# Three sizes of expert tile, mixing weights split in another stage, and a later split of the S5 rows, in a one-layer hybrid decoder kernel

## The reference

```python
h = rms_norm(x, g_mix); proj = h @ w_in            # q, k, v of 3 head groups | S5 input | gate_a | gate_b
attn = dilated_window_attention(...)               # 3 groups (window 128, 512, 2048; dilation 1, 4, 16), 8 heads of 64
y_a = attn @ w_attn_proj                           # groups combined per position by their softmax denominators
y_s = gelu(s5_ssm(u)); y_s = y_s * sigmoid(y_s @ w_glu + b_glu)
x = x + (sigmoid(gate_a) * y_a + sigmoid(gate_b) * (y_s @ w_ssm_proj)) @ w_out
h2 = rms_norm(x, g_ffn)
top_v, top_i = top_k(h2 @ w_router + b_router, 4)  # 4 of 32 experts for each token
gu = rows_of_expert @ w_gu + b_gu                  # 1024 -> 2 x 1024, per expert
act = min(g, 7) * sigmoid(1.702 * min(g, 7)) * (clip(l, -7, 7) + 1)
x[token] += gate * (act @ w_down + b_down)         # 1024 -> 1024
```

## Time and profile before

| | us |
|---|---|
| median of 3 runs | 5875.7 (5872.85 to 5878.38) |
| the profiled execution | 5878.18, with a span of 5876.5 |
| TensorE busy | 5454.7 (93% of the span) |
| VectorE busy | 3167.2 (54%) |
| ScalarE busy | 1765.4 (30%) |
| GpSimd busy | 990.3 (17%) |

### The profile page before, as it was taken

One profiled execution on the slowest core, in us unless ns is written; L12 is line 12 of the kernel. 1 busy time (PEld: TensorE's weight loads), 2 busy tenths in 40 slices (PEclk: granted clock), 3 DMA queues, 4 the chain that ended last, 5 costly groups with the idle time before them and its releaser, 6 DMA issues.

```text
span 5876.5 us, 81957 instructions
## 1 busy us (share of the span) xinstructions
PE 5454.7 (93%) x30240; PEld 4852.6 (83%) x30240; DVE 3167.2 (54%) x5833; ACT 1765.4 (30%) x2783; POOL 990.3 (17%) x813
## 2 busy tenths in 40 slices
PE   8999999959979986869699999999999999999997
PEld 7888888848857884658699999999999899999997
DVE  4323220016655665535456566565665777777776
ACT  4111111101105672113223233233333343434343
POOL 0000000003300001213213222132221222222222
PEclk9999999975559997989799999999999999999999
DMA  3122122110012334344444445444454666666665
GB/s 135 67 77 74 67 77 74 67 61 1 0 52 107 115 128 165 127 148 143 150 144 154 162 142 175 143 155 167 137 174 143 218 214 215 224 217 219 220 220 191
DMA packets 237817, 803.35 MB, mean 137 GB/s; under 512 B 32534, under 2 KB 52654, under 8 KB 201808
## 3 DMA queue, kind: packets, MB, share of 16 engines
q1 hardware_dynamic: 198960, 673.20, 31.2%
q0 software_dynamic: 32944, 107.67, 8.0%
q10 hardware_dynamic: 5760, 20.45, 1.1%
HBM read 652.88 MB, written 148.94 MB: 136 GB/s over the span
## 4 chain that ended last, share of the span: by engine, by line
PE 45%; DVE 4%; ACT 1%; issue 1%; DMA 0%; POOL 0%; DVEq 0%; ACTq 0%; POOLq 0%
PE ex_g L1905 28%; PE ex_d L1919 15%; DVE ex_y L2050 2%; PE ex_g L1891 1%; ACT ex_wgh L1956 1%; DVE ex_wdl L2008 1%; DVE ex_wgl L2002 1%; DVE ex_t L2029 0%; DVE ex_bgu L2023 0%; POOL ex_y L1863 0%; DMA ex_nxt<-slots_d 0%; DMA ex_xg<-h_d,ex_nxt 0%; ACT ex_xh L1969 0%; POOL out L1866 0%; DVEq L2059 0%
## 5 line engine op out<-in xcount | busy, mean ns | idle before, releaser
L1905 PE MATMUL ex_g<-ex_xh,ex_wgh 128*128 128x256 f32 (+1 forms) x4352 | 1341.3, 308 | 56.9 <-DVE ex_t L2029 49.5
L1905 PE MATMUL ex_g<-ex_xh,ex_wgl 128*128 128x256 f32 (+1 forms) x4352 | 1334.6, 307 | 0.0
L1905 PE MATMUL ex_g<-ex_xl,ex_wgh 128*128 128x256 f32 (+1 forms) x4352 | 1334.0, 307 | 0.0
L1905 PEld LDWEIGHTS ex_g<-ex_xh,ex_wgh 128*128 128x128 f32 x4352 | 820.2, 188 | 87.5 <-issue 57.0
L1905 PEld LDWEIGHTS ex_g<-ex_xl,ex_wgh 128*128 128x128 f32 x4352 | 820.2, 188 | 8.6
L1905 PEld LDWEIGHTS ex_g<-ex_xh,ex_wgl 128*128 128x128 f32 x4352 | 821.1, 189 | 0.0
L2002 DVE TENSOR_TENSOR ex_wgl<-ex_wg,ex_wgh 128x2048 fp32r<-128x2048 f32 x274 | 626.6, 2287 | 55.8 <-ACT ex_wgh L1956 53.5
L1956 ACT ACTIVATE ex_wgh<-ex_wg 128x2048 fp32r<-128x2048 f32 x274 | 524.6, 1915 | 436.0 <-PE ex_g L1905 409.4
L1863 POOL TENSOR_SCALAR ex_y<-ex_y,ex_cur 128x1024 f32<-128x1024 f32 x84 | 298.3, 3551 | 1712.3 <-DVE ex_y L2050 1712.3
L1919 PE MATMUL ex_d<-ex_wdh,ex_ath 128*128 128x512 f32 x1344 | 538.6, 401 | 0.0
L1919 PE MATMUL ex_d<-ex_wdl,ex_ath 128*128 128x512 f32 x1344 | 530.4, 395 | 0.0
(11 more groups left out here) (343 smaller groups left out, 8767.0 us busy)
## 6 DMA issues: line engine op xcount, KB each, us to landing
ex_wg<-in_w_gu SPq DMA_DIRECT2D x276, 1024.0 KB, 4.8
ex_wd<-in_w_down SPq DMA_DIRECT2D x276, 512.0 KB, 5.6
qkv_d<-prj_o SPq DMA_DIRECT2D x144, 256.0 KB, 2.0
att_blk<-qkv_d SPq DMA_DIRECT2D x48, 768.0 KB, 4.2
prj_raw<-in_w_in SPq DMA_DIRECT2D x112, 256.0 KB, 3.7
ex_bd<-in_b_down SPq DMA_DIRECT2D x34, 512.0 KB, 6.6
gate_d<-prj_o SPq DMA_DIRECT2D x64, 256.0 KB, 2.0
mix_ring<-gate_d SPq DMA_DIRECT2D x32, 512.0 KB, 3.7
```

Of the source, the lines that this page charges most:

```text
L1905: last = pe.matmul(gu[j][:, 0:size], w[:, k, j, :], x[:, k, 0:size], start=(k == 0 and x is xh and w is h), stop=(k == KD - 1 and w is l))
```

## The change

There are three parts.

1. **Experts.** A third tile size, MIDDLE = 320. An expert's rows are cut into large tiles as long as more than 512 remain beyond them. Of the rest, over 384 gives two tiles of 256, 321 to 384 one of 384, 257 to 320 one of 320, up to 256 one of 256. The table has one more column (the first tile of the third kind), each engine loads one more number and runs three loops. In a middle tile the gate-up product and the elementwise work on its result have 320 columns; everything counted in groups of 128 rows has three groups, as in a large tile.
2. **Mixing weights.** The ten pieces are loaded, copied and subtracted during attention: SyncE issues a load in every second block, behind the load of a block, and GpSimd makes the high and the low part in the odd blocks, behind the copy of kT. The six weight tiles live from attention to the end of mixing. The ring, ScalarE and VectorE have no weight pieces in the mixing stage any more, the first chunk's order is written anew, and the loads of attention results are issued ahead of the S5 rows.
3. **S5 rows.** In the mixing chunks `split_y(c + 1)` moves on VectorE from ahead of column block 0 to ahead of column block 3, and on ScalarE behind the second save.

The diff, cut: the same edits (a third loop, `n0, n1, n`, `TW` for 4) repeat on the other engines; waits on the weight pieces are dropped in `glu`, `product` and the ring.

```diff
-LARGE, SMALL = 384, 256
+LARGE, MIDDLE, SMALL = 384, 320, 256
 NGT = LARGE // P
 REGION = -(-S // LARGE) * LARGE
 SLOTS = NE * REGION + LARGE
 DUMP = S + LARGE
+TW = 5
...
+                    if n % 2 == 0 and n // 2 < len(pieces):
+                        r = n // 2
+                        if r >= PR:
+                            sp.wait_ge(low, r - PR + 1)
+                        sp.dma_start(raw[r % PR][:, :], pieces[r][0]).then_inc(raw_in[r % PR], 16)
                     g, row, step, _ = blocks[n]
                     sp.wait_ge(o_saved, n + 1)
                     sp.dma_start(att_d[g, row:row + (P - 1) * step + 1:step, :],
@@ -923,6 +932,13 @@
                         if n:
                             pool.wait_ge(s_mm, PB * n)
                         pool.tensor_copy(kT[(n + 1) % 2][:, :, 0:P], kT[n % 2][:, :, P:2 * P]).then_inc(k_kept, 1)
+                    if n % 2 and n // 2 < len(pieces):
+                        r = n // 2
+                        _, h, l = pieces[r]
+                        pool.wait_ge(raw_in[r % PR], 16 * (r // PR) + 16)
+                        pool.tensor_copy(h, raw[r % PR][:, :]).then_inc(high, 1)
+                        pool.wait_ge(high, r + 1)
+                        pool.tensor_tensor(l, raw[r % PR][:, :], h.bitcast(F32), ALU.subtract).then_inc(low, 1)
...
-                def load_piece(n):
-                    src, k = pieces[n][2:]
-                    if n >= GR:
-                        sp.wait_ge(wl_ready, n - GR + 1)
-                    src = src[:, k:k + 2, :] if n < KA // 2 else src[:, k, :].rearrange("p (h n) -> p h n", h=2)
-                    sp.dma_start(ring[n % GR][:, :, :], src).then_inc(ring_in[n % GR], 16)
                 def load_gates(t):
                     c, o = divmod(t, NO)
-                    r = (NP + t) % GR
-                    if t < GR:
-                        sp.wait_ge(wl_ready, NP + t - GR + 1)
-                    else:
+                    r = t % GR
+                    if t >= GR:
...
+                load_att(0)
                 load_y(0)
-                load_piece(0)
-                load_piece(1)
-                load_att(0)
                 load_att(1)
                 sp.dma_start(bg[:, :], b_glu).then_inc(bg_in, 16)
-                for n in range(2, NP):
-                    load_piece(n)
...
+                turn(0)
                 glu(0)
-                for n in range(NBLK):
+                for n in range(1, NBLK):
...
+                weigh(0)
                 split_y(0)
-                split_weights(0)
-                split_weights(1)
                 act.wait_ge(bg_in, 16)
-                weigh(0)
-                for n in range(2, 4):
-                    split_weights(n)
+                weigh(1)
+                save(0)
                 gate(0)
-                weigh(1)
-                for n in range(4, NP):
-                    split_weights(n)
-                save(0)
                 weigh(2)
                 save(1)
                 weigh(3)
                 save(2)
                 save(3)
                 for c in range(NCH - 1):
-                    split_y(c + 1)
                     weigh(NBLK * (c + 1))
                     for j in range(NBLK):
                         if j + 1 < NBLK:
                             weigh(NBLK * (c + 1) + j + 1)
                         save(NBLK * (c + 1) + j)
+                        if j == 1:
+                            split_y(c + 1)
                     gate(c + 1)
             @block.vector
             def _(dve):
                 tt = dve.tensor_tensor
-                def split_weights(n):
-                    dve.wait_ge(wh_ready, n + 1)
-                    tt(piece(1, n), ring[n % GR][:, :, :].rearrange("p k n -> p (k n)"), piece(0, n).bitcast(F32),
-                       ALU.subtract).then_inc(wl_ready, 1)
...
+                combine(0)
                 split_y(0)
-                split_weights(0)
-                split_weights(1)
-                combine(0)
-                for n in range(2, 4):
-                    split_weights(n)
+                combine(1)
+                save(0)
                 gate(0)
-                combine(1)
-                for n in range(4, NP):
-                    split_weights(n)
-                save(0)
                 combine(2)
                 save(1)
                 combine(3)
@@ -1379,7 +1347,7 @@
                 for c in range(NCH):
                     more = c + 1 < NCH
                     for o in range(NO):
-                        if more and o == 0:
+                        if more and o == 3:
...
-                full, part = both[:, 0:NE], both[:, NE:2 * NE]
-                dve.memset(junk[:, 0:2 * NE], 1.0)
+                full, middle, small = (both[:, n * NE:(n + 1) * NE] for n in range(3))
+                dve.memset(junk[:, 0:3 * NE], 1.0)
                 chain(dve.tensor_copy(cnt[:, :], pr[:, 0:NE]))
-                chain(tsc(full, cnt[:, :], float(SMALL), None, ALU.is_gt))
+                chain(tsc(full, cnt[:, :], 2.0 * SMALL, None, ALU.is_gt))
                 for j in range(1, REGION // LARGE):
-                    chain(stt(full, cnt[:, :], float(SMALL + j * LARGE), full, ALU.is_gt, ALU.add))
-                chain(stt(part, full, -float(LARGE), cnt[:, :], ALU.mult, ALU.add))
-                chain(tsc(part, part, 0.0, None, ALU.is_gt))
-                chain(dve.tensor_tensor_scan(upto[:, :], junk[:, 0:2 * NE], both[:, :], 0.0, ALU.mult, ALU.add))
+                    chain(stt(full, cnt[:, :], 2.0 * SMALL + j * LARGE, full, ALU.is_gt, ALU.add))
+                chain(stt(cnt[:, :], full, -float(LARGE), cnt[:, :], ALU.mult, ALU.add))
+                tsc(two[:, :], cnt[:, :], float(LARGE), None, ALU.is_gt)
+                tsc(middle, cnt[:, :], float(SMALL), None, ALU.is_gt)
+                chain(tsc(mask[:, :], cnt[:, :], float(MIDDLE), None, ALU.is_gt))
+                chain(stt(small, cnt[:, :], 0.0, middle, ALU.is_gt, ALU.subtract))
+                tt(full, full, mask[:, :], ALU.add)
+                chain(stt(small, two[:, :], 2.0, small, ALU.mult, ALU.add))
+                tt(middle, middle, mask[:, :], ALU.subtract)
+                chain(tt(full, full, two[:, :], ALU.subtract))
+                chain(dve.tensor_tensor_scan(upto[:, :], junk[:, 0:3 * NE], both[:, :], 0.0, ALU.mult, ALU.add))
                 chain(tsc(before[:, :], upto[:, :], row[:, :], None, ALU.is_le))
                 chain(dve.tensor_reduce(ei[:, :], before[:, :], AX.X, ALU.add))
                 chain(tt(before[:, :], before[:, :], upto[:, :], ALU.mult))
                 chain(dve.tensor_reduce(nth[:, :], before[:, :], AX.X, ALU.max))
                 chain(tt(nth[:, :], row[:, :], nth[:, :], ALU.subtract))
-                chain(tsc(second[:, :], ei[:, :], float(NE), -float(NE), ALU.is_ge, ALU.mult))
-                chain(tt(second[:, :], ei[:, :], second[:, :], ALU.add))
-                chain(tsc(tail[:, :], ei[:, :], -float(NE), None, ALU.add))
+                tsc(later[:, :], ei[:, :], float(NE), None, ALU.is_ge)
+                chain(tsc(last_[:, :], ei[:, :], 2.0 * NE, None, ALU.is_ge))
+                chain(stt(second[:, :], later[:, :], -float(NE), ei[:, :], ALU.mult, ALU.add))
+                chain(stt(second[:, :], last_[:, :], -float(NE), second[:, :], ALU.mult, ALU.add))
+                chain(stt(tail[:, :], later[:, :], float(NE), second[:, :], ALU.mult, ALU.add))
+                chain(tsc(tail[:, :], tail[:, :], -float(NE), None, ALU.add))
                 chain(tsc(before[:, 0:NE], ecol[:, :], tail[:, :], None, ALU.is_equal))
                 chain(tt(before[:, 0:NE], before[:, 0:NE], full, ALU.mult))
                 chain(dve.tensor_reduce(tail[:, :], before[:, 0:NE], AX.X, ALU.add))
-                chain(tt(nth[:, :], nth[:, :], tail[:, :], ALU.add))
-                chain(tsc(nth[:, :], nth[:, :], float(LARGE), None, ALU.mult))
+                chain(tsc(later[:, :], later[:, :], float(SMALL - LARGE), float(LARGE), ALU.mult, ALU.add))
+                chain(tt(nth[:, :], nth[:, :], later[:, :], ALU.mult))
+                chain(stt(nth[:, :], tail[:, :], float(LARGE), nth[:, :], ALU.mult, ALU.add))
                 chain(stt(tab[:, 1:2], second[:, :], float(REGION), nth[:, :], ALU.mult, ALU.add))
                 chain(tsc(tab[:, 1:2], tab[:, 1:2], float(NE * REGION), None, ALU.min))
                 tsc(tab[:, 0:1], second[:, :], float(NE - 1), None, ALU.min)
                 chain(tsc(tab[:, 2:3], upto[:, NE - 1:NE], 1.0, None, ALU.max))
-                chain(tsc(nth[:, :], tab[:, 2:3], 1.0, None, ALU.add))
-                chain(tt(tab[:, 3:4], upto[:, 2 * NE - 1:2 * NE], nth[:, :], ALU.max))
+                for n in (1, 2):
+                    chain(tsc(nth[:, :], tab[:, n + 1:n + 2], 1.0, None, ALU.add))
+                    chain(tt(tab[:, n + 2:n + 3], upto[:, (n + 1) * NE - 1:(n + 1) * NE], nth[:, :], ALU.max))
...
```

(27 more changed lines are left out.)

81 lines of the change are left out of this document (37 added, 44 removed).

## The result

The changed kernel takes 5676.1 us (median of 4 runs, 5673.9 to 5681.1), the kernel before 5876.1 (4 runs, 5872.9 to 5878.4). The ratio is 0.966, with a 95% interval of 0.9646 to 0.9674. The forecast was 5666.

A forecast was written before the change was run, and what follows sets the result against it. TensorE was taken to bound the expert stage, waits the mixing stage. 168.0 - 5 + 49.3 - 3 = 209.3 us off the profiled 5878.2 gave 5668.9, less 2.5 for the median 5666; range 18 below up to 5706.

The forecast's parts named there:

- three signs: Signs of error: middle boundaries at clock 0.50, kT copies ending after scores could start, a 320-column product over 7.3 us.
- Columns and tiles: Expert stage: 3 large, 11 middle, 20 small tiles; 102.9 us from middle tiles plus 65.1 from two turned small, 168.0 together.
- Rival (c): Expert gate-up: 320 columns cost as much as 384, 103 us more, 5769; chance 0.04.
- Rival (f): Expert tiles: routing counts differ from the list or a tile isn't made, up to 168 us lost, 5834; chance 0.01.
- Clock at the middle boundaries: Expert tiles: 2.3 us idle at each middle tile may drop TensorE's clock, 0 to 32 us for eleven; 5 taken.
- Rival (a): Expert stage: the clock falls at every middle tile, 27 us more, 5693; chance 0.14.
- Mixing, start: Mixing stage up to the first weighing: 29 us gained without the weight pieces, bounds 20 to 32.
- Mixing, chunks: Mixing chunk heads: moving the S5 split saves 27.2 us and costs 6.9 on VectorE, a gain of 20.3.
- TensorE's 249 us of work leave room: Mixing stage: TensorE's work leaves room for a stage of 291 us, with 49.3 us gained in all.
- Attention: GpSimd's weight pieces take 3.8 us each, loads land 3.9 us after issue, 3.3 us to spare: cost 0.
- The bound for blocked VectorE, 38 us: Attention: if GpSimd blocked VectorE for 3.8 us in each of ten pieces, 38 us; 0 taken.
- Small costs: Table operations ahead of the experts 2.4 us, one more number and three more semaphores 0.6: 3 in all, bounds 1 and 6.

The follow-up runs named there:

- experiment 3: Changed kernel with the middle size set to 256, so loads of 257 to 320 take a large tile: 5771.1 us, ratio 0.9814.
- the first profile: The first profiled execution of the changed kernel, with nothing further altered: 5676.8 us.
- the repeat: The changed kernel profiled once more with nothing altered, as a control: 5671.8 us.
- experiment 8: Changed kernel with attention's raw piece of mixing weights issued ahead of the block load instead of behind it: 5672.0 us, ratio 0.9649.
- Experiment 4: Changed kernel with VectorE's split of the next chunk's S5 rows behind, not ahead of, the combination in output block 3: 5665.0 us, ratio 0.9638.
- experiment 1: Kernel before with only the new tile sizes, table and expert loops; mixing weights and S5 splits as before: 5714.7 us, ratio 0.972.
- experiment 6: Changed kernel with a copy of 768 columns and a wait for it on VectorE before every tile's first clamp: 5697.2 us, ratio 0.9691.
- experiment 10: Changed kernel with the tile loop started later by one or three VectorE copies, and once unaltered: 5676.4, 5678.1 and 5671.8 us.
- experiment 9: Changed kernel with biases read ahead, first down split deferred, VectorE's S5 split behind the combination and raw piece issued first: 5609.5 us, ratio 0.9543.
- experiment 5: Changed kernel with VectorE's two bias operations for the next tile moved to the last strip of the tile before: 5639.4 us, ratio 0.9593.

## Why the prediction was right, and where it was off

The time, 5676.1, is 10 over the forecast and inside the range; every gain had the right sign, and one cost put at nothing wasn't nothing. Two of the three signs that the prediction named as making it wrong did show, middle boundaries with a granted clock of 0.50 and late copies of kT; both cost less than they could have, and the total came near partly because errors of both signs met in it. By its own steps:

- **Columns and tiles: right.** 3, 11 and 20 tiles; 7.03 us for 6.985; 94.90 us a middle tile for 94.91. Rival (c), by which 320 would cost as much as 384, is out by the chain, and experiment 3 gives the price of eleven middle tiles as 95.0 us. The two large tiles turned small follow (104.3 and 71.6). Rival (f) is out by the counts.
- **Clock at the middle boundaries: right mechanism, mis-sized.** The idle time was 2.19 us (2.3 foretold). The sum had 5 us; the falls cost 7.5, as 5 tiles times 1.5 (4 to 6 tiles in the other runs with this idle time). I had priced a fall by the 2.9 us behind the 3.52 us; behind the 2.19 us each cost half. The length doesn't fix the cost either: behind 3.51 us it was 2.7 us in the first profile and 1.3 in the repeat. Rival (a), a fall each time, didn't come, even at 2.79 us. The Trainium skill, "TensorE: Matmul & The Clock Gate", section "HAM oscillation — how this bites in real kernels", tells of a loop that waits 3 to 5 us for a transfer in each pass and falls every time; the waits here are 2.19 us, so the prediction took that section further than it goes when it made the whole 32 due by it. The trace agrees in part: the fall comes back from tile to tile, but in 5 passes of 11. The first tile took 1.4 us more than before, which is within its spread (experiment 8).
- **Mixing, start: right.** First weighing 51.6 us behind the first load (53 foretold), a gain of 30.8 for 29.
- **Mixing, chunks: the step that failed.** The sum had 27.2 - 6.9 = 20.3 and 13.1 came. The heads gave 24.7 (VectorE's small two-input operation behind GpSimd's addition stretches the first combination by 1.2 us at each). The split costs 6.6, near the 6.9: each is 3.07 and not 2.29 us long, but the next combination's first small operation, 0.95 us before, takes 0.16 behind it. What I had left out is the clock: the split makes TensorE wait 4.06 us for the fourth combination, and behind that wait the clock fell in all three chunks, 6.5 us. The kernel before had lost 1.5 of them at the same stretch of its first chunk, so 5.0 are new: 24.7 - 6.6 - 5.0 = 13.1. Experiment 4 shortens the wait to 1.86 us, and the falls shrink to 3.1 us but don't go. "TensorE's 249 us of work leave room" was true of its work and said nothing of its clock.
- **Attention: cost 0 became 1.7.** GpSimd's piece is 3.4 us (3.8 foretold), but its load lands 5.5 us after the issue in the median, not the 3.9 that I took from a ring of the mixing stage; that is the mis-sized term. Experiment 8 shows it: landings of 4.1, and the loss is gone. The bound for blocked VectorE, 38 us, was far off, for the reason given.
- **Small costs:** 3 foretold, 0.6 measured between last weighing and first gate-up. The 0.6 in the sum for one more number and three more semaphores stands in no row, and no run measured it by itself.

Together: chunks +7.2, attention and its end +2.2, experts +2.7, start -1.8, small costs -2.4, which is 7.9 of 8.0 in the span; the other 2 are how the profiled executions lie to the medians, and rounding. The forecast of -163 us for the expert stage met -160.3, and experiment 1 met it alone.

**Open:** what decides, at 1.8 to 2.8 us of idle time, whether the clock falls behind it. It isn't the length alone (experiment 6) nor the program (experiment 10). How the falls are spread over a run is read here, not explained. Nor is it shown why a fall behind one idle time costs 1.3 us in one run and 2.7 in another. The length of the first expert tile is also a matter of clock (0.60 in its first 8 us, 0.81 before) that no experiment aimed at.

## What to carry to other kernels

When one engine's matmuls get shorter, read what hides under the next wait: the last of the eight products saved nothing, and what it didn't fill became idle time and a risk for the clock. Price a wait of TensorE twice, as its length and as the slow stretch that may stand behind it, also in a stage that TensorE doesn't bound. And when the order of a queue is the bound, look at all that is queued in front of the operation that others wait for: two small bias operations, 0.16 us each where GpSimd leaves them alone and 0.8 and 0.7 where it doesn't, were worth 36.7 us in 34 tiles, more than the whole reordering of the chunk heads (27.7).

## What the runs showed of the hardware

- **Idle time and clock.** Falls of the granted clock behind TensorE's idle time. At tile boundaries: 0.98 us, none; 1.26 and 1.39, none of 30; 1.84, 1 to 3 in each run, of 17 or 19; 2.19, 4 to 6 of 11 in each of eight runs; 2.43, 5 of 19; 2.79, 2 of 11; 2.58 (once), 3.5 and 4.1, each time. In the mixing chunks, at the fourth combination: 4.06, three of three; 1.86, two of three in experiment 4 and three of three in experiment 9. A fall costs 1.3 to 2.9 us.
- **Held operations.** VectorE's subtraction of 2048 columns took 3.07 us for 2.28 when GpSimd's addition ran beside its start; one of 256 columns 2.75 for 0.42 beside GpSimd's scatter and scaling; one of 8 columns up to 1.43 us for 0.17. These three read two SBUF tiles. The Trainium skill, "SBUF — State Buffer", section "SBUF: two separate sides", says that such an operation and GpSimd's lock each other out for an instruction's whole length; the 2.75 us row agrees in kind. The two bias operations of 8 columns, which read one SBUF tile each, were held too: 0.79 and 0.73 us beside GpSimd's scaling, 0.16 each in experiment 5.
- **Matmul columns.** One gate-up matmul in the chain: 117.7, 146.5 and 173.3 ns at 256, 320 and 384 columns (5.65, 7.03 and 8.32 us for 48). The cost is linear in the columns to 1%.
